# Compressed branch in four column groups, and three moves of turns and projection ends, in a two-model kernel

## What is computed

```python
# first model, per layer
x = x + 0.5 * swiglu(rms_norm(x), ...)
z = rms_norm(x) @ w_in                 # rq rk rv rg | mq mk mv | ca cg
y = concat(retention(rq, rk, rv) gated by silu(rg), causal_attention(mq, mk, mv), conv31(ca, cg))
x = x + y @ w_out
x = x + 0.5 * swiglu(rms_norm(x), ...)
# second model, per layer: mixer with a compressed, selected and windowed branch,
# a dilated branch and a forgetting branch
kc = compress(k_cmp, 0); vc = compress(v_cmp, 1)
def compress(t, j):                    # 15 blocks of 32 tokens x 64 = 2048 values each
    blk = t[:, cmp_idx] + cmp_pe[j]
    hid = silu(blk.reshape(B, 15, 2048) @ cmp_w1[j])      # 2048 -> 128
    return hid @ cmp_w2[j]                                # 128 -> 64
```

## Time and profile before

| | us |
|---|---|
| median of 3 runs | 2198.03 (2195.98 to 2198.46) |
| the profiled execution, its own time | 2196.24 |
| its span in the profile | 2194.4 |
| PE busy | 2175.4 |
| DVE busy | 1515.8 |
| ACT busy | 1116.1 |

### The profile page before, as it was taken

How to read it: one execution, slowest core, us unless ns; L and a number is a source line. 1 busy time by engine, 2 the same in 40 slices (tenths; PEclk the granted TensorE clock), 3 DMA queues, 4 the chain that set the end, 5 groups by cost and what they waited for, 6 DMA issues and landing times.

```text
span 2194.4 us, 26673 instructions
## 1 busy us (share of the span) xinstructions
PE 2175.4 (99%) x10710; PEld 1818.6 (83%) x10710; DVE 1515.8 (69%) x2313; ACT 1116.1 (51%) x1735; POOL 25.8 (1%) x32
## 2 busy tenths in 40 slices
PE   8999999999999999999999999999999999999998
PEld 7888888888888888888888987888888889778887
DVE  5655974456875977877876555888688766558565
ACT  5445654444445654445445666544454456655443
POOL 0000010000000010000000000000000000000000
PEclk9999999999999999999999999999999999999999
DMA  8554454556884457876876444688768864445653
GB/s 300 193 199 149 151 181 172 192 199 216 284 299 157 158 184 267 282 258 208 280 277 215 144 150 134 201 272 276 267 226 285 285 198 157 145 136 186 226 201 125
DMA packets 252800, 462.91 MB, mean 211 GB/s; under 512 B 11958, under 2 KB 58080, under 8 KB 252548
## 3 DMA queue, kind: packets, MB, share of 16 engines
q1 hardware_dynamic: 252276, 460.85, 62.0%
q10 hardware_dynamic: 400, 0.36, 0.1%
HBM read 460.12 MB, written 1.05 MB: 210 GB/s over the span
## 4 chain that ended last, share of the span: by engine, by line
PE 91%; DVE 6%; ACT 2%; issue 0%; DMA 0%; POOL 0%; SPq 0%; POOLq 0%; DVEq 0%; ACTq 0%
PE ps L1894 18%; PE ps L1897 18%; PE ps L1895 18%; PE s L1894 8%; PE s L1897 8%; PE s L1895 8%; PE ps L1864 4%; DVE wl L2544 2%; DVE cacc L2772 1%; PE s L2042 1%; PE ps L1910 1%; PE ps L1908 1%; PE ps L1909 1%; PE ps L2068 1%; DVE gts L2945 1%; ACT pt L2342 1%
## 5 line engine op out<-in xcount | busy, mean ns | idle before, releaser
L2544 DVE TENSOR_TENSOR wl<-raw,wh 128x1024 fp32r<-128x1024 f32 (+2 forms) x740 | 856.1, 1186 | 132.3 <-ACT wh L2235 128.2
L2235 ACT ACTIVATE wh<-raw 128x1024 fp32r<-128x1024 f32 (+2 forms) x740 | 731.6, 1031 | 393.1 <-PE ps L1897 127.1
L1894 PE MATMUL ps<-wh,xh 128*128 128x512 f32 (+3 forms) x1600 | 615.0, 384 | 0.4 <-DVE wl L2544 0.4
L1897 PE MATMUL ps<-wh,xl 128*128 128x512 f32 (+3 forms) x1600 | 604.2, 378 | 0.1
L1895 PE MATMUL ps<-wl,xh 128*128 128x512 f32 (+3 forms) x1600 | 603.9, 377 | 0.0
L1894 PEld LDWEIGHTS ps<-wh,xh 128*128 128x128 f32 x1600 | 300.8, 188 | 57.1 <-issue 9.7
L1897 PEld LDWEIGHTS ps<-wh,xl 128*128 128x128 f32 x1600 | 300.5, 188 | 48.8 <-DVE xl L2589 0.5
L1895 PEld LDWEIGHTS ps<-wl,xh 128*128 128x128 f32 x1600 | 301.0, 188 | 45.5
L2552 DVE SCALAR_TENSOR_TENSOR acc<-raw,condT,acc 128x512 f32<-128x512 f32 x252 | 188.8, 749 | 5.1
L2335 ACT ACTIVATE hTh<-ps 128x512 fp32r<-128x512 f32 x88 | 48.3, 596 | 219.0 <-PE ps L1864 219.0
L2696 DVE TENSOR_TENSOR hTl<-ps,hTh 128x512 fp32r<-128x512 f32 x88 | 57.1, 687 | 139.9 <-ACT hTh L2335 139.8
(11 more groups left out here) (370 smaller groups left out, 2426.7 us busy)
## 6 DMA issues: line engine op xcount, KB each, us to landing
raw<-in_ffn_w_in SPq DMA_DIRECT2D x80, 1024.0 KB, 5.4
raw<-in_ada_w SPq DMA_DIRECT2D x72, 1024.0 KB, 6.0
raw<-in_ffn_wu SPq DMA_DIRECT2D x40, 1024.0 KB, 5.8
raw<-in_ffn_wd SPq DMA_DIRECT2D x40, 1024.0 KB, 5.5
raw<-in_ffn_w_out SPq DMA_DIRECT2D x40, 1024.0 KB, 6.1
raw<-in_ffn_wg SPq DMA_DIRECT2D x39, 1024.0 KB, 5.3
raw<-in_mix_w_in SPq DMA_DIRECT2D x28, 1024.0 KB, 5.2
raw<-in_w_in SPq DMA_DIRECT2D x28, 768.0 KB, 4.5
```

What stands on the lines that cost most here:

```text
L1894: e.matmul(o, X[0](kk, t), hi, start=kk == 0, stop=False)
L1897: ins = e.matmul(o, X[1](kk, t), hi, start=False, stop=kk == K - 1 or (banks[t], kk) == self.closed)
L2235: ins = self.e.activation(m.wh[j % NH][:, 0:n], m.raw[u % NR][:, k0 * w:k0 * w + n], ACT.Copy)
L2544: ins = self.e.tensor_tensor(m.wl[j % NH][:, 0:n], m.raw[u % NR][:, k0 * w:k0 * w + n], hi, ALU.subtract)
```

## The change

1. The first layer of the compressed branch runs in four column groups: keys and values, each in two halves of the sum, to four banks (two turning banks, 4 and 5). The halves are copied out without Silu, two by ACT and two by DVE, into one tile that DVE has zeroed; two matmuls with halves of the identity turn and add them; one Silu of 128x64 follows.
2. The turns of the dilated queries come one sub-step later, behind the hidden layer and directly ahead of that turn.
3. In the first mixer rq's turns go to bank 7, then 6, and turn_wo(0) goes to bank 6.
4. In attention of the first mixer a projection that ends in the first half of a loop is finished (taps, copies, rotation) behind the values.

```diff
@@ -1108,6 +1108,7 @@   (attention)
         for g in range(n + 1):
+            self.held = None if short else []
             if g:
                 self.turn(groups[g - 1])
...
                 if g and half == 0 and groups[g - 1].pairs:
                     self.values(groups[g - 1])
+                for done, b, tk in self.held or ():
+                    done(b, tk)
+                self.held = None
@@ -1245,7 +1249,10 @@   (fill)
                 self.jobs.pop(0)
-                j["done"](j["b"], tk)
+                if self.held is None:
+                    j["done"](j["b"], tk)
+                else:
+                    self.held.append((j["done"], j["b"], tk))
@@ -1349,7 +1356,11 @@   (mix1, q_done)
                 def post():
+                    t = self.tbank
+                    if n == "rq":
+                        self.tbank = 6
                     rdy[n] = self.heads_out(m.qk[n], zi, r)
+                    self.tbank = t
@@ -1477,6 +1488,7 @@   (mix1)
         ret_out(2)
+        self.tbank = 7
         turn_wo(0)
@@ -1570,9 +1582,9 @@   (mix2, n1_done)
-            def post_dq():
+            def turn_dq():
                 rdy["dq"], self.zt_free[1] = self.turn_heads(lambda i, t: z1[:, t, (i + 1) * P:(i + 2) * P], 3, m.qk["dq"], [rq])
-            self.post(post_dq, LAG + 1)
+            held.append(turn_dq)
@@ -1648,18 +1660,17 @@   (mix2)
-        bb = (self.next_t(), self.next_t())
+        bb = (self.next_t(), self.next_t(), 4, 5)
         self.cmp_hidden(l, bb)
...
-        for kv in range(2):
-            self.free[bb[kv]] = (s.act, ("hid", l, kv))
+        for g in range(4):
+            self.free[bb[g]] = (s.act if g < 2 else s.vec, ("hid", l, g))
         self.fill()
-        bb = (self.next_t(), self.next_t())
-        self.cmp_turn(l, bb)
-        for kv in range(2):
-            self.free[bb[kv]] = (s.act, ("hidT", l, kv))
+        held.pop()()
+        self.cmp_turn(l, 4)
+        self.free[4] = (s.act, ("hidT", l))
         self.fill()
@@ -2145,24 +2156,27 @@   (PE: cmp_hidden, cmp_turn)
-        for j in range(16):
-            for kv in range(2):
-                ins = self.e.matmul(m.ps[bb[kv]][32 * kv:32 * kv + 15, 0:P], blk[kv][:, j, :], w1[kv][:, j, :],
-                                    start=j == 0, stop=j == 15)
+        self.wait_ge(*[self.free[b] for b in bb])
+        for j in range(8):
+            for g in range(4):
+                half, kv = divmod(g, 2)
+                n = 8 * half + j
+                ins = self.e.matmul(m.ps[bb[g]][32 * g:32 * g + 15, 0:P], blk[kv][:, n, :], w1[kv][:, n, :],
+                                    start=j == 0, stop=j == 7)
...
-            ins = self.e.transpose(m.ps[bb[kv]][:, 0:15], m.pt[kv][r, 512:640], m.ident[r, r])
+        for half in range(2):
+            ins = self.e.matmul(m.ps[b][:, 0:64], m.pt[0][:, 512:640], m.ident[:, 64 * half:64 * half + 64],
+                                start=half == 0, stop=half == 1)
@@ -2452,17 +2466,15 @@   (ACT: cmp_hidden, cmp_turn)
-            self.then_inc(self.e.activation(m.pt[kv][r, 512:640], m.ps[bb[kv]][r, 0:P], ACT.Silu), (self.s.act, ("hid", l, kv)))
+            self.then_inc(self.e.activation(m.pt[0][r, 512:640], m.ps[bb[g]][r, 0:P], ACT.Copy), (self.s.act, ("hid", l, g)))
...
-            self.then_inc(self.e.activation(m.small[:, 128 + 32 * kv:143 + 32 * kv], m.ps[bb[kv]][:, 0:15], ACT.Copy),
-                          (self.s.act, ("hidT", l, kv)))
+        self.then_inc(self.e.activation(m.small[:, 128:192], m.ps[b][:, 0:64], ACT.Silu), (self.s.act, ("hidT", l)))
@@ -2875,7 +2887,8 @@   (DVE: cmp_blocks, cmp_hidden)
-        e.memset(m.small[:, 128:192], 0.0)
+        self.wait_ge(self.pt_free[0])
+        self.then_inc(e.memset(m.pt[0][:, 512:640], 0.0), (s.vec, ("hid0", l)))
...
+    def cmp_hidden(self, l, bb):
+        m, s, e = self.m, self.s, self.e
+        self.wait_ge((s.prod, ("cmp1", l)), (s.vec, ("hid0", l)))
+        for g in (2, 3):
+            r = slice(32 * g, 32 * g + 15)
+            self.then_inc(e.tensor_copy(m.pt[0][r, 512:640], m.ps[bb[g]][r, 0:P]), (s.vec, ("hid", l, g)))
```

More of the change, by code:

```diff
@@ L431, in __init__ @@
         self.rt_free, self.gab_free, self.col_free = None, [None, None], [None, None, None]
-        self.jobs, self.posts = [], []
+        self.jobs, self.posts, self.held = [], [], None
         self.foxb_free, self.x_sum = None, None
@@ L1611, in mix2 @@
         gtok, gated, sigmoids = {}, {}, [False]
-        w1_free = []
+        w1_free, held = [], []
         def mg_done(i):
@@ L1798, in cmp_hidden, with cmp_turn @@
         pass
-    def cmp_turn(self, l, bb):
+    def cmp_turn(self, l, b):
         pass
@@ L2147, in cmp_hidden, with cmp_turn @@
         for kv in range(2):
-            self.wait_ge((self.s.w1[kv], 16 * (l + 1)), (self.s.vec, ("blk", l, kv)), self.free[bb[kv]])
-        for j in range(16):
-            for kv in range(2):
-                ins = self.e.matmul(m.ps[bb[kv]][32 * kv:32 * kv + 15, 0:P], blk[kv][:, j, :], w1[kv][:, j, :],
-                                    start=j == 0, stop=j == 15)
+            self.wait_ge((self.s.w1[kv], 16 * (l + 1)), (self.s.vec, ("blk", l, kv)))
+        self.wait_ge(*[self.free[b] for b in bb])
[5 more added lines that the diff above has]
+                                    start=j == 0, stop=j == 7)
         self.then_inc(ins, (self.s.prod, ("cmp1", l)))
-    def cmp_turn(self, l, bb):
+    def cmp_turn(self, l, b):
         m = self.m
-        for kv in range(2):
-            r = slice(32 * kv, 32 * kv + 15)
-            self.wait_ge((self.s.act, ("hid", l, kv)), self.free[bb[kv]])
-            ins = self.e.transpose(m.ps[bb[kv]][:, 0:15], m.pt[kv][r, 512:640], m.ident[r, r])
+        self.wait_ge(*[(self.s.act if g < 2 else self.s.vec, ("hid", l, g)) for g in range(4)], self.free[b])
+        for half in range(2):
+            ins = self.e.matmul(m.ps[b][:, 0:64], m.pt[0][:, 512:640], m.ident[:, 64 * half:64 * half + 64],
+                                start=half == 0, stop=half == 1)
         self.then_inc(ins, (self.s.turned, ("hidT", l)))
@@ L2164, in cmp_kv @@
         m, s, e = self.m, self.s, self.e
-        self.wait_ge((s.act, ("hidT", l, 1)), (s.misc, 160), self.free[b])
+        self.wait_ge((s.act, ("hidT", l)), (s.misc, 160), self.free[b])
         e.matmul(m.ps[b][:, 0:15], m.w2d[:, l, 0:2, :].rearrange("p a f -> p (a f)"), m.small[:, 128:143],
@@ L2454, in cmp_hidden, with cmp_turn @@
         m = self.m
-        for kv in range(2):
-            r = slice(32 * kv, 32 * kv + 15)
-            self.wait_ge((self.s.prod, ("cmp1", l)), self.pt_free[kv])
-            self.then_inc(self.e.activation(m.pt[kv][r, 512:640], m.ps[bb[kv]][r, 0:P], ACT.Silu), (self.s.act, ("hid", l, kv)))
-    def cmp_turn(self, l, bb):
+        self.wait_ge((self.s.prod, ("cmp1", l)), (self.s.vec, ("hid0", l)))
+        for g in range(2):
+            r = slice(32 * g, 32 * g + 15)
+            self.then_inc(self.e.activation(m.pt[0][r, 512:640], m.ps[bb[g]][r, 0:P], ACT.Copy), (self.s.act, ("hid", l, g)))
+    def cmp_turn(self, l, b):
         m = self.m
         self.wait_ge((self.s.turned, ("hidT", l)))
-        for kv in range(2):
-            self.then_inc(self.e.activation(m.small[:, 128 + 32 * kv:143 + 32 * kv], m.ps[bb[kv]][:, 0:15], ACT.Copy),
-                          (self.s.act, ("hidT", l, kv)))
+        self.then_inc(self.e.activation(m.small[:, 128:192], m.ps[b][:, 0:64], ACT.Silu), (self.s.act, ("hidT", l)))
     def cmp_scores(self, l, qn):
@@ L2886, in cmp_blocks, with cmp_turn @@
                           (s.vec, ("blk", l, kv)))
-    def cmp_turn(self, l, bb):
+    def cmp_hidden(self, l, bb):
         m, s, e = self.m, self.s, self.e
-        self.wait_ge((s.act, ("hidT", l, 1)))
+        self.wait_ge((s.prod, ("cmp1", l)), (s.vec, ("hid0", l)))
+        for g in (2, 3):
+            r = slice(32 * g, 32 * g + 15)
+            self.then_inc(e.tensor_copy(m.pt[0][r, 512:640], m.ps[bb[g]][r, 0:P]), (s.vec, ("hid", l, g)))
+    def cmp_turn(self, l, b):
+        m, s, e = self.m, self.s, self.e
+        self.wait_ge((s.act, ("hidT", l)))
         self.then_inc(e.tensor_copy(m.ptT[0][:, 256:384].rearrange("p (h n) -> p h n", h=4),
```

## The result

| | before | changed |
|---|---|---|
| median of the runs | 2196.82 us (20 runs, 2195.85 to 2199.15) | 2199.80 us (20 runs, 2197.61 to 2203.73) |
| profiled execution, span | 2194.4 us | 2197.2 us |
| its mean granted clock | 0.999 | 0.998 |

The ratio is 1.0015, with a 95% interval of 1.0008 to 1.0021. The forecast was 2199.0 us and no change beyond 0.2%, and that is what came. The interval leaves out 1, so the change is a small loss, of some 3 us. It also leaves out the forecast's own ratio, 1.0005: the loss is larger than the 1.0 us forecast. The profiles of the two executions differ by the same 2.8 us.

A forecast was written before the change was run, and what follows sets the result against it. PE, busy 2175.4 of 2194.4 us, was taken as the bound, with DVE nearly full in first mixers. Profiled 2196.24 - 4.4 (second mixers) + 5.4 (first mixers) = 2197.2, plus 1.79 to the median: 2199.0 us; range 2190 to 2203.

The forecast's parts named there:

- Four column groups, 3.5 us in two layers, and the wait for pt, 1.1: Second mixers, compressed first layer: 1.75 us gained per layer, plus PE's 0.56 us wait for ACT's Silu copies removed.
- no better than two: Rival, second mixers: only two column groups ever run at once, giving back 3.5 us, 2202.5 us; chance 0.08.
- the rival of weight loads: Rival, second mixers: 64 loads of 96 ns can't hide under matmuls, +4.4 us per layer, 2207.8 us; chance 0.04.
- The margin ahead of Silu: Second mixers: Silu out near 1225.9, its reader starts near 1226.2, 0.3 us to spare.
- Holding the ends of projections: First mixers: DVE idles 1.7 and 2.1 us before y1l, making PE 3.3 us late at retention's next scores.
- turn_wo(0) in bank 6: First mixers: PE's 0.56 us wait for ACT to empty the bank goes, about 0.6 us gained per mixer.
- The 0.25 us for rq's banks: First mixers: the values need only the first copy of Trq, 0.25 us sooner, if Trq comes no later.
- four steps: First mixers: y1l delays the taps, then masks, exponentials and Trq, then the second split, then decays and retention's scores.
- The wait for Trq: First mixers: the second group's values start at about 261.9 instead of 260.36, their wait 1.5 us longer.
- +2.7 us per mixer, in two: First mixers: PE 3.3 us late less 0.6 us gained at turn_wo, the same in both layers, +5.4 us.
- The first mixers gain too: Rival: y1l waits under 0.5 us at each place, 1.35 us gained per first mixer, 2190.9 us; chance 0.25.
- The slack in DVE is smaller still: Rival, first mixers: each DVE hole reaches PE in full, +0.65 us per mixer more, 2200.3 us; no separate chance given.

## Why the prediction was right, and where not

*What bounds the kernel.* Right. PE is busy for 99% of the span in both profiles, and the gains and losses were found as waits of PE or as a shorter stage on PE.

*Four column groups, 3.5 us in two layers, and the wait for pt, 1.1.* Right: 4.6 us measured for this part alone, 4.4 forecast, and 2.2 us in each second mixer by the table of the changed kernel. The stage took 1.87 us where 1.75 and the next start were expected. The rival "no better than two" is refuted. So is the rival of weight loads: 64 loads of 96 ns are 6.1 us, and all lay within a stage of 1.87. The rule quoted from the Trainium skill ("TensorE: Matmul & The Clock Gate", Part 3, The mechanism), by which a load overlaps with matmuls in flight only if the row group differs, doesn't hold for these matmuls, which use all rows and differ in the column group; the measurement decides. The margin ahead of Silu was half of what I took (0.16 us for 0.3), which cost nothing here, but is thin.

*Holding the ends of projections.* Right in mechanism and nearly in size. Idle before y1l: 1.7 and 2.1 us forecast, 1.54 and 2.05 seen. The second scores of retention in layer 0: PE 3.3 us late forecast, 4.07 - 0.99 = 3.08 seen. For the whole mixer 2.7 was forecast and 2.69 seen in layer 0. That it is so exact is in part luck, for two terms were too large and cancel: holding cost 3.1 us per mixer and not 3.3, and turn_wo(0) in bank 6 gave 0.4 and not 0.6. The 0.25 us for rq's banks showed in the wait of the values and came to nothing at the end of the mixer. The forecast followed the queue through four steps; a mere "DVE has 1.4 us of slack" would not have given this. The wait for Trq was to become 1.5 us longer and went from 0.39 to 1.94 us. The wait for the decays was shorter than in the kernel with holding alone (0.8 us for 1.3), probably because the slow clock had used some of that time.

*What the prediction missed: layer 1 is not layer 0.* "+2.7 us per mixer, in two" is the step that failed. I followed the banks in layer 0 only. The toggle, once exchanged by `self.tbank = 7`, was still exchanged in layer 1, and there the mixer cost 3.58 us and not 2.7. Setting it back removed the wait of 1.79 us from the profile and 0.94 us from the mixer; the other 0.85 us of that wait had stood in place of the one for the decays. With it set back the two mixers cost 2.69 + 2.64 = 5.3 us, and the forecast had 5.4.

*The sum.* +1.0 us was forecast against the profiled execution; +2.8 came, of which 0.99 is the late start and 0.9 the exchanged toggle in layer 1; what is left agrees with the forecast. By the medians the change costs 3.0 us, 1.1 more than by the profiles, and no run shows where that lies. It is in part luck that the time itself, 2199.0 us, is only 0.8 us off. It was counted from the median of three runs, 2198.03, and twenty runs of the same kernel have 2196.82: a start 1.2 us too high and a change 2 us too small. "Within 0.2%" was right with 1.4 us of room; the upper end of the interval, 1.0021, is just beyond the bound.

*The other rivals.* "The first mixers gain too" is what comes once the taps go first, though not to the 2190.9 us worked out for it: 2192.26 us with the taps at once and the toggle set back, where each first mixer gains 0.75 us and not 1.35. "The slack in DVE is smaller still", at 2200.3 us, is as near to the measured median as the forecast is, but PE's 3.08 us at the second scores speak against it: they are less than the 3.3 of the forecast, where this rival wanted more.

## What to carry to other kernels

On an engine that executes in order, an instruction that waits costs what is ready behind it. When work is moved behind a waiting instruction, look for pieces of it that need nothing from what is waited for, and leave those ahead: here letting the ready taps go first was worth 7.7 us by the medians, 6.8 by the profiles of the first mixers. Do it by following the queue through the timeline, once for each layer, for a toggle of buffers that one edit shifts stays shifted for everything that comes later. And where small matmuls use few columns, four column groups ran four at the price of one, weight loads included.

## What the runs showed of the hardware that was not expected

The granted clock fell. In the changed kernel PE waits 1.94 us for Trq, starts the values at 262.69, and at 263.55 the clock goes to half (1.2 of 2.4 GHz) for 3.41 us; the same in layer 1 at 758.48. One stretch by the windows (the number behind the four busy engines and POOL is the granted clock), and the matmuls at that time:

```profile
264.00:265.00 1.00, 1.00 (x5) 1.00 (x4) 0.00 (x0) 1.00 (x4) 0.00 (x0) 0.50 0.87 272
```
```profile
264.59 0.53 PE L1905 MATMUL ps<-wh,xh 128*128 128x384 f32 x1
264.91 0.53 PE L1906 MATMUL ps<-wl,xh 128*128 128x384 f32 x1
...
267.43 0.33 PE L1906 MATMUL ps<-wl,xh 128*128 128x384 f32 x1
267.61 0.33 PE L1908 MATMUL ps<-wh,xl 128*128 128x384 f32 x1
```

At half clock one starts every 0.32 us instead of every 0.174, 0.146 us lost on each of the ten or eleven there, 1.5 to 1.6 us in all. In the profiled execution that didn't reach the end: PE's next scores start when DVE is through with the decays, PE still waited 0.83 us for them after the slow stretch, and DVE's own chain hangs on the values, which had started before the clock fell. The kernel with holding alone bears this out: its profile has no such fall, and yet holding costs it 3.1 us in each first mixer, as much as in the changed kernel, where the clock fell in both. So the fall is not what makes holding dear.

The fall belongs to holding. The mean clock was 0.999 or 1.000 in all runs of the versions without holding and in all those of the kernel before that were timed beside the experiments, in 25 of 26 of those that hold but let the taps go first or leave some out, and 0.997 or 0.998 in 19 of 20 runs of the changed kernel and in 8 of 11 with the toggle set back. In the kernel with holding alone it was 0.998 in five of six runs (mean 2204.35 us); the sixth, at 0.999, is the fastest (2201.95 us) and is the one in the profile, whose 2.2 us waits were followed by no fall. So after the same wait the clock sometimes falls and sometimes doesn't; what decides it was not tried. Nor is its price settled in the runs that have no profile. That one run is 2.4 us below the mean of the other five, which the slow stretches may have cost, or the start of the program, which differs by as much between the profiles. In the changed kernel the nine runs at 0.997 have a mean of 2201.07 us, the ten at 0.998 one of 2199.45, and the one at 0.999 took 2201.92; with the toggle set back there is no such order. The spread is wider too: the changed kernel's runs lie within 6.1 us, those of the kernel before within 3.3.
